# Two transformer layers on one core: the norm roots, the split order and GpSimd's products at three stage beginnings

## What is computed

```python
def rmsnorm(x, g):
    return x * rsqrt(mean(x * x, axis=-1) + EPS) * g

h = h + mix @ w_o                                             # end of the first layer's mixing
n = rmsnorm(h, g_ffn)
h = h + (silu(n @ w_gate) * (n @ w_up)) @ w_down              # feed-forward 1
x = rmsnorm(h, g_final)                                       # between the layers
hn = rms_norm(x, attn_norm_g); proj = hn @ w_in_2             # second layer begins
h = x + mixed @ w_out_2
hn = rms_norm(h, ffn_norm_g)
h = h + (silu(hn @ w_gate_2) * (hn @ w_up_2)) @ w_down_2      # feed-forward 2
```

## Time and profile before

| | |
|---|---|
| median of 3 runs | 797.39 us (796.32 to 799.02) |
| profiled execution | 796.91 us, its span 795.2 us |
| granted TensorE clock, mean | 0.996 |
| busy: PE, PEld | 757.7 us (95%), 680.0 us |
| busy: DVE, ACT, POOL | 530.1, 421.0, 73.9 us |
| DMA read | 129.39 MB, 165 GB/s over the span |
| chain that ended last: PE, DVE, ACT, POOL | 58%, 8%, 2%, 1% of the span |

### The profile page before, as it was taken

How to read it: one execution, slowest core, us unless ns; L and a number is a source line. 1 busy time by engine, 2 the same in 40 slices (tenths; PEclk the granted TensorE clock), 3 DMA queues, 4 the chain that set the end, 5 groups by cost and what they waited for, 6 DMA issues and landing times.

```text
span 795.2 us, 12591 instructions
## 1 busy us (share of the span) xinstructions
PE 757.7 (95%) x4989; PEld 680.0 (86%) x4989; DVE 530.1 (67%) x930; ACT 421.0 (53%) x799; POOL 73.9 (9%) x106
## 2 busy tenths in 40 slices
PE   2999999999999998999999998998989999999998
PEld 2999999989989987888888887997768888888886
DVE  5666465766555768777457757687877877547762
ACT  5356655455554446665345546468455555436551
POOL 8000000013022001000000003301500000000000
PEclk9999999999999999999999999999999999999999
DMA  9887636334433465564656563643234655665521
GB/s 289 237 262 236 164 68 185 107 107 116 150 107 134 159 212 164 181 206 167 211 179 192 187 202 98 214 146 114 102 119 145 212 185 186 212 196 175 168 97 54
DMA packets 108410, 132.04 MB, mean 166 GB/s; under 512 B 4267, under 2 KB 97513, under 8 KB 108352
## 3 DMA queue, kind: packets, MB, share of 16 engines
q1 hardware_dynamic: 106048, 126.56, 49.9%
q0 software_dynamic: 2304, 4.68, 2.6%
HBM read 129.39 MB, written 1.84 MB: 165 GB/s over the span
## 4 chain that ended last, share of the span: by engine, by line
PE 58%; DVE 8%; ACT 2%; issue 2%; POOL 1%; POOLq 0%; DVEq 0%
PE B L1480 23%; PE B L1457 19%; PE B L1462 10%; PE B L1441 5%; DVE LO L902 3%; ACT HI L510 1%; POOL SGC L465 1%; DVE AA L908 0%; PE B L1487 0%; PE B L1616 0%; DVE TMP L1358 0%; ACT SGC L830 0%; DVE NW L918 0%; ACT AA L514 0%; DVE ST L1177 0%
## 5 line engine op out<-in xcount | busy, mean ns | idle before, releaser
L902 DVE TENSOR_TENSOR LO<-RAW,HI 128x1024 fp32r<-128x1024 f32 x240 | 282.5, 1212 | 118.1 <-ACT HI L510 117.6
L510 ACT ACTIVATE HI<-RAW 128x1024 fp32r<-128x1024 f32 x240 | 237.8, 1040 | 60.1 <-PE B L1480 55.3
L1457 PE MATMUL B<-AA,HI 128*128 128x512 f32 x704 | 243.8, 399 | 2.6 <-DVE SGC L1191 2.1
L1480 PE MATMUL B<-HI,AA 128*128 128x512 f32 (+1 forms) x800 | 211.6, 350 | 6.4 <-DVE AA L1374 3.8
L1441 PE MATMUL B<-AA,HI 128*128 128x256 f32 (+1 forms) x992 | 186.0, 289 | 3.5 <-DVE LO L902 1.7
L1462 PE MATMUL B<-AA,LO 128*128 128x256 f32 x704 | 183.2, 281 | 0.0
L1480 PEld LDWEIGHTS B<-HI,AA 128*128 128x128 f32 x800 | 141.5, 190 | 26.3 <-DVE AA L1374 4.2
L1441 PEld LDWEIGHTS B<-AA,HI 128*128 128x128 f32 (+1 forms) x992 | 156.4, 193 | 5.7 <-DVE LO L902 2.1
L1457 PEld LDWEIGHTS B<-AA,HI 128*128 128x128 f32 x704 | 126.8, 188 | 27.9 <-DVE SGC L1191 2.7
L1441 PE MATMUL B<-AA,LO 128*128 128x256 f32 (+1 forms) x496 | 141.4, 285 | 0.0
L1462 PEld LDWEIGHTS B<-AA,LO 128*128 128x128 f32 x704 | 132.9, 189 | 8.1
(11 more groups left out here) (276 smaller groups left out, 639.0 us busy)
## 6 DMA issues: line engine op xcount, KB each, us to landing
RAW<-in_w_in SPq DMA_DIRECT2D x30, 1024.0 KB, 6.2
RAW<-in_w_gate SPq DMA_DIRECT2D x22, 1024.0 KB, 5.3
RAW<-in_w_up SPq DMA_DIRECT2D x22, 1024.0 KB, 5.3
RAW<-in_w_down SPq DMA_DIRECT2D x22, 1024.0 KB, 5.0
RAW<-in_w_in SPq DMA_DIRECT2D x9, 512.0 KB, 6.4
RAW<-in_w_attn_out SPq DMA_DIRECT2D x4, 1024.0 KB, 5.3
RAW<-in_w_o SPq DMA_DIRECT2D x4, 1024.0 KB, 5.0
RAW<-in_w_out SPq DMA_DIRECT2D x4, 1024.0 KB, 5.2
```

What stands on the lines that cost most here:

```text
L510: e.activation(pieces(HI, NSPL, i, k), pieces(RAW, NRAW, i, k), ACT.Copy).then_inc(split_hi, 1)
L902: e.tensor_tensor(pieces(LO, NSPL, i, k), pieces(RAW, NRAW, i, k), pieces(HI, NSPL, i, k), ALU.subtract).then_inc(split_lo, 1)
L1457: return e.matmul(dst[:, :], hi[:, t, c0:c0 + 128], flatten(AA[:, ch + t, :, :]), start=(t == 0), stop=(t == nk - 1))
L1480: x = e.matmul(dst, a, w[:, t, c0:c0 + n], start=(first and t == 0 and k == 0), stop=(last and t == nk - 1 and k == 2))
```

## The change

Five things are edited:
1. Four roots (one at the beginning of each feed-forward part, two at the beginning of the second layer) are no longer computed by DVE's `rsqrt`. DVE counts up `mean_sb`, and GpSimd raises the 128x2 tile to the power -0.5 in one instruction (`root`, a new constant tile ROOT), counts up `root_sb`, and DVE goes on. The two roots at the very start of the kernel stay as they were.
2. GpSimd's G2 product waits for `fg_sb` 6 (the third gate unit of feed-forward 1), its two X products wait for `diag_sb` 4 (the diagonals at the beginning of the second layer).
3. In both feed-forward parts the split of unit g+3 for i = 0 moves behind the two banks' copies, on ACT and on DVE.
4. At the beginning of the second layer the split of unit U_TWO+1 moves behind the last two turned halves, on ACT and on DVE.
5. There DVE's split of unit U_TWO+2, whose halves lay between the parts of the root, moves behind the diagonals.

To have semaphores free, `bias_out` and `bias_in` are made one, and so are the pairs of the two gates' semaphores (`gate_pe`, `gate_tanh`, `gate_sb`), with values that go on counting; nothing waits for another event than before by that. The diff without these renamings:

```diff
+        ROOT = sb("ROOT", [128, 2])
...
             e.memset(ones[:, :], 1.0).then_inc(setup, 1)
+            e.memset(ROOT[:, :], -0.5).then_inc(setup, 1)
...
+            def root(n, dst, src):
+
+                e.wait_ge(mean_sb, n)
+                e.tensor_tensor(dst, src, ROOT[:, :], ALU.pow).then_inc(root_sb, 1)
+
...
             e.wait_ge(scaled_sb, 8)
             gain(1, A["attn_norm_g_2"][0, :])
+            e.wait_ge(setup, HALF)
+            root(1, ST[:, 6:8], ST[:, 4:6])
             e.wait_ge(gain_in[0], 32)
             e.wait_ge(gain_in[1], 32)
             e.wait_ge(mix_lo, 8)
+            e.wait_ge(fg_sb, 6)
             e.tensor_tensor(G2, GB[:, 0, :], GB[:, 1, :], ALU.mult).then_inc(gain2, 1)
...
-            e.wait_ge(factor1, 1)
+            root(2, ST[:, 6:8], ST[:, 4:6])
+            root(3, ST[:, 26:28], ST[:, 24:26])
+            e.wait_ge(root_sb, 2)
             e.wait_ge(squares_sb, 16)
             e.wait_ge(final_x, 4)
+            e.wait_ge(diag_sb, 4)
             for t in range(2):
                 e.tensor_scalar(X[:, t, :], TOK[:, t, :], ST[:, 6 + t:7 + t], None, ALU.mult).then_inc(normal_x, 1)
...
             mean(1, bufs[1][:, 0:256], bufs[2], bufs[0])
+            root(4, ST[:, 6:8], ST[:, 4:6])
...
                     g = ffn_unit(first, "gate", i)
                     hi(g + 2)
-                    if i == 0:
-                        hi(g + 3)
...
-                    if i > 0:
-                        hi(g + 3)
+                    hi(g + 3)
...
+                for t in range(2):
+                    turned(12 + 2 * h + t, B[5 + t], 4 * h, t)
                 if h == 1:
                     hi(U_TWO + 1)
-                for t in range(2):
-                    turned(12 + 2 * h + t, B[5 + t], 4 * h, t)
...
-                    if h == 1 and split is not None:
-                        lo(split)
                     if targets:
                         for t in range(2):
                             turned(n + 2 * h + t, B[5 + t], 4 * h, t)
+                    if h == 1 and split is not None:
+                        lo(split)
...
-            def factor(nsq):
+            def factor(nsq, n):
                 e.wait_ge(squares_sb, nsq)
-                own.step(e.scalar_tensor_tensor(ST[:, 4:6], ST[:, 0:4:2], EPS, ST[:, 1:4:2], ALU.add, ALU.add))
-                own.step(rsqrt(ST[:, 6:8], ST[:, 4:6], 2))
-                own.wait()
+                e.scalar_tensor_tensor(ST[:, 4:6], ST[:, 0:4:2], EPS, ST[:, 1:4:2], ALU.add, ALU.add).then_inc(mean_sb, 1)
+                e.wait_ge(root_sb, n)
                 diagonals(ST[:, 6:8])
...
                     lo(g + 2)
-                    if i == 0:
-                        lo(g + 3)
...
-                    if i > 0:
-                        lo(g + 3)
+                    lo(g + 3)
...
             e.wait_ge(squares_sb, 16)
-            own.step(e.scalar_tensor_tensor(ST[:, 4:6], ST[:, 0:4:2], EPS, ST[:, 1:4:2], ALU.add, ALU.add))
-            rsqrt(ST[:, 6:8], ST[:, 4:6], 2).then_inc(factor1, 1)
-            lo(U_TWO + 2, 0)
+            e.scalar_tensor_tensor(ST[:, 4:6], ST[:, 0:4:2], EPS, ST[:, 1:4:2], ALU.add, ALU.add).then_inc(mean_sb, 1)
             own.step(e.tensor_tensor(ST[:, 24:26], ST[:, 20:24:2], ST[:, 21:24:2], ALU.add))
-            e.wait_ge(factor1, 1)
+            e.wait_ge(root_sb, 2)
             for _ in range(2):
                 own.wait()
                 own.step(e.tensor_tensor(ST[:, 24:26], ST[:, 24:26], ST[:, 6:8], ALU.mult))
             own.wait()
-            own.step(e.tensor_scalar(ST[:, 24:26], ST[:, 24:26], EPS, None, ALU.add))
-            own.step(rsqrt(ST[:, 26:28], ST[:, 24:26], 2))
-            own.wait()
+            e.tensor_scalar(ST[:, 24:26], ST[:, 24:26], EPS, None, ALU.add).then_inc(mean_sb, 1)
+            e.wait_ge(root_sb, 3)
             e.tensor_tensor(ST[:, 28:30], ST[:, 26:28], ST[:, 6:8], ALU.mult).then_inc(factor2, 1)
-            lo(U_TWO + 2, 1)
             e.wait_ge(factor2, 1)
             diagonals(ST[:, 28:30])
+            lo(U_TWO + 2)
```

More of the change, by code:

```diff
@@ L170, in program @@
         conv_hi, conv_lo = sem("conv_hi"), sem("conv_lo")
[L171 removed]
+        gate_pe, gate_tanh = sem("gate_pe"), sem("gate_tanh")
         co_pe, co_sb = sem("co_pe"), sem("co_sb")
@@ L179, in program @@
         fu_pe, fu_low, fu_sb, ff_sb, ff_hi, ff_lo = (sem(n) for n in ("fu_pe", "fu_low", "fu_sb", "ff_sb", "ff_hi", "ff_lo"))
-        factor1, factor2 = sem("factor1"), sem("factor2")
+        mean_sb, root_sb, factor2 = sem("mean_sb"), sem("root_sb"), sem("factor2")
         tm_pe, tm_sb, fm_pe, fm_sb = sem("tm_pe"), sem("tm_sb"), sem("fm_pe"), sem("fm_sb")
@@ L234, in program @@
         for i in range(4):
-            cols(w1, GBO + 48 + 256 * i, 256, gc_pe, 2 * i + 2)
+            cols(w1, GBO + 48 + 256 * i, 256, gate_pe, 2 * i + 2)
         for i in range(2):
@@ L238, in program @@
         for i in range(4):
-            cols(w1, GBO + 48 + 1024 + 256 * i, 256, ga_pe, 2 * i + 2)
+            cols(w1, GBO + 48 + 1024 + 256 * i, 256, gate_pe, 2 * i + 10)
         for i in range(4):
@@ L397, in _, with gates @@
             e.dma_start(bias_rows.rearrange("h r n -> h (r n)").rearrange("h (r n) -> h r n", n=ROW),
-                        OH[0:4, :].unsqueeze(1).to_broadcast([4, 128, ROW])).then_inc(bias_out, 16)
-            def gates(dst, tanh, done):
+                        OH[0:4, :].unsqueeze(1).to_broadcast([4, 128, ROW])).then_inc(bias_moved, 16)
+            def gates(dst, first):
                 for ch in range(8):
-                    e.wait_ge(tanh, ch + 1)
-                    e.tensor_scalar(dst[:, ch, :], dst[:, ch, :], 0.5, 0.5, ALU.mult, ALU.add).then_inc(done, 1)
+                    e.wait_ge(gate_tanh, first + ch + 1)
+                    e.tensor_scalar(dst[:, ch, :], dst[:, ch, :], 0.5, 0.5, ALU.mult, ALU.add).then_inc(gate_sb, 1)
                     yield
@@ L623, in turned_weights, with gates @@
                 e.activation(PT[:, s % 2, :], B[5 + s % 2][:, :], ACT.Copy).then_inc(pturn_sb, 1)
-            def gates(dst, u, pe, done):
+            def gates(dst, u, first):
                 for i in range(4):
@@ L629, in gates @@
                         ch = 2 * i + c
-                        e.wait_ge(pe, ch + 1)
-                        e.activation(dst[:, ch, :], B[c][:, 0:S], ACT.Tanh, scale=0.5).then_inc(done, 1)
+                        e.wait_ge(gate_pe, first + ch + 1)
+                        e.activation(dst[:, ch, :], B[c][:, 0:S], ACT.Tanh, scale=0.5).then_inc(gate_tanh, 1)
                         yield
@@ L662, in fill @@
                 e.wait_ge(block_lo, 1)
-                yield from gates(SGC, u, gc_pe, gc_tanh)
+                yield from gates(SGC, u, 0)
                 u = U_FILL + 12
@@ L671, in fill @@
                 e.wait_ge(o_pe, o_no(13))
-                yield from gates(SGA, u, ga_pe, ga_tanh)
+                yield from gates(SGA, u, 8)
             filler = fill()
@@ L1225, in _ @@
             lo(U_FF1 + 1)
-            factor(8)
+            factor(8, 1)
             ffn(U_FF1, 0, 1)
@@ L1297, in second_most @@
                 if i == 0:
-                    e.wait_ge(bias_in, 16)
+                    e.wait_ge(bias_moved, 32)
                 if i >= 2:
@@ L1410, in _ @@
             lo(U_FF2 + 1)
-            factor(20)
+            factor(20, 4)
             ffn(U_FF2, 22, 3)
@@ L1623, in turn_outputs, with gates @@
                     turn(4 + 2 * h + t, TOK[:, t, halves(h)], 5 + t)
-            def gates(u, pe, tanh):
+            def gates(u, first):
                 for ch in range(8):
-                    take(ch % 2, tanh, ch + 1)
-                    stationary(u + ch // 2, 128 * (ch % 2), B[ch % 2][:, 0:S], 0, ch % 2 == 0).then_inc(pe, 1)
+                    take(ch % 2, gate_tanh, first + ch + 1)
+                    stationary(u + ch // 2, 128 * (ch % 2), B[ch % 2][:, 0:S], 0, ch % 2 == 0).then_inc(gate_pe, 1)
                     yield
@@ L1651, in fill @@
                         yield
-                yield from gates(U_FILL + 8, gc_pe, gc_tanh)
+                yield from gates(U_FILL + 8, 0)
                 e.wait_ge(conv_lo, 4)
@@ L1658, in fill @@
                         yield
-                yield from gates(U_FILL + 14, ga_pe, ga_tanh)
+                yield from gates(U_FILL + 14, 8)
             e.wait_ge(q_sb, 8)
```

17 lines of the change are left out of this document (8 added, 9 removed).

## The result

The changed kernel takes 790.55 us (median of 4 runs, 790.15 to 790.96), the kernel before beside it 796.99 us (4 runs, 796.32 to 799.02): a ratio of 0.9915, 95% interval 0.9896 to 0.9934, so 5.3 to 8.3 us less. The forecast was 791.5 us.

A forecast was written before the change was run, and what follows sets the result against it. PE, busy for 95% of the 795.2 us span, bounds the kernel, so its waits count. Gains of 2.69 + 0.73 + 2.56 - 0.15 = 5.83 us from 796.91, with 0.48 added for the median, give 791.5 us; range 789.8 to 795.3.

The forecast's parts named there:

- Feed-forward 1: At its beginning the diagonals end at 305.42 + p; PE's waits before spread and gate unit 1 go, gain 2.69 us.
- The step on gate unit 1: Feed-forward 1: with only two half splits ahead of the bank B0 sum, the 1.35 us wait goes if p is under 3.4.
- G2's new place: Near 330 us in feed-forward 1, G2 keeps DVE out for up to 2.8 us; never late, costed at nothing.
- Feed-forward 2: At its beginning the bank B0 sum comes earlier and PE's wait before gate unit 1 goes: gain 0.73 us.
- Turned halves: Second layer's beginning: copies go ahead of U_TWO+1's split; PE's wait of 2.56 us goes, but for 0.1 at most.
- The roots of the second layer: Second layer's beginning: U_TWO+2's split ends at 499.2 + 2p + w; 2p + w must stay under 1.7 us.
- p: Time of one power on POOL at each of the four moved roots, taken as 0.5 us.
- w: Second layer's beginning: time the X products keep DVE out of U_TWO+2's split, taken as 0.85 us, bounds 0 and 1.7.
- the term of -0.15 us: A new PE wait of 0.15 us at U_TWO+2 in the second layer, from 2p + w = 1.85, taken off the gain.
- The price formula for a slow power: Rival at all four roots: above 2.7 us waits grow by p - 2.7, 2p - 0.85, p - 2.5; gain 12.0 - 4p; chance 0.08.
- The rivals: X products hold DVE out fully, 0.17; power moderately long, 0.12; time comes back elsewhere, 0.06; slow power routine, 0.08.
- The sum: Whole kernel: the gains at the three stage beginnings, 2.69 + 0.73 + 2.56 - 0.15 = 5.83 us.

The follow-up runs named there:

- the roots alone: The kernel before with only the four roots moved to GpSimd, order of before, neither added wait: 796.6 us, ratio 0.9976 to the kernel before.
- the run with four powers: The changed kernel with each of the four roots computed four times in series on GpSimd: 796.87 us, ratio 0.9986 to the kernel before.
- the second (7.3 to 9.4): The changed kernel, with nothing further changed, measured once more against the kernel before: 790.23 us, ratio 0.9895.

## Why the prediction was right, step by step

- **Feed-forward 1, right.** The mean takes 0.15 us, both waits are gone. The diagonals end at 308.19, 1.54 us after the mean's start at 306.65; the formula gives 0.15 + 0.22 + 0.72 + 0.48 = 1.57 us. The gain was 3.17 and not 2.69 us, since a wait costs more than its bracket here. The step on gate unit 1 gave its wait to edit 3; the runs show that the short root with G2 held back does it alone and that edit 3 does it alone too. The number does not depend on it, since both are in the change.
- **G2's new place, right in effect.** That G2 would keep DVE out near 330 us at no cost is what happened (L1204 takes 2.94 us for two there, and PE does not wait). What the prediction did not say is what G2 would have done in its old place behind the power: the roots alone keep 1.52 us of the two waits for it. The held product is part of the change and not of the prediction's reasons for the gain.
- **Feed-forward 2, right.** 0.96 us instead of 0.73, for the same reason.
- **Turned halves, right.** 2.57 us of 2.56. PE has no gap at all, where up to 0.1 was allowed.
- **The roots of the second layer, right, with two errors that in part cancel.** p is 0.7 and not 0.5 us, and w, the time that the X products take from U_TWO+2's split, is 0 and not 0.85. DVE's part of U_TWO+2 ends at 496.49 + 2.35 = 498.8; the formula with p = 0.7 and w = 0 gives 500.6 in the time of the execution before, 499.5 in this one's, which is 1.1 us ahead there. So 0.7 us more slack than was worked out, and the term of -0.15 us fell away. The size of w was right and its place was wrong. An X product does keep DVE out for some 0.85 us, but here the first half of U_TWO+2's split begins before it and the second follows without a break, both at their usual 1.22 us; the time falls on the first half of U_TWO+3's split (1.53 us instead of 0.68), for which PE does not wait. With the roots alone, where the second half of U_TWO+2's split begins 0.12 us behind the first X product, that half takes 2.07 us instead of 1.22: so w can fall on this split. (In the earlier trace rows the row of 1.01 us is two instructions, of 0.82 and 0.16 us, so the first hold there was 0.66 us.) POOL's two products grew from 6.58 to 9.65 us. The rule of the Trainium skill (SBUF — State Buffer, "Who interferes with whom") that the one that holds the port locks out the other for its whole instruction is borne out for the TENSOR_TENSOR G2; the TENSOR_SCALAR X products, 4.71 and 4.95 us long, did not keep DVE's splits out for their whole length.
- **The price formula for a slow power, right but for that slack.** With p = 3.04 us it gives waits of 0.34, 0.54 and (2p - 1.7, w = 0) 4.4 us, in all 5.3; the trace has 0.35, 0.27 and 3.65, the last one shorter by the same 0.7 us of slack. The formula's break-even is at 3.0 us, and there the run with four powers lies, with a ratio of 0.9986. It loses some clock besides, so part of that agreement is chance.
- **The rivals.** None took place at the power's real length. The Trainium skill (GPSIMD Engine Reference, "Instruction dispatch") has about 6 us for the first call of a freshly loaded routine; the first power here takes 0.72 us, the later ones 0.69 to 0.72.
- **The sum.** 5.83 forecast; by the starts of rows 6.7. The missing part is 0.24 us for each of three waits and the 0.15 that was taken off for nothing. The first comparison (5.3 to 8.3 us) holds 5.83, the second (7.3 to 9.4) does not: the sum has no term for the clock, and the gain was somewhat larger than forecast.

## What to carry to other kernels

A chain of small instructions on a busy engine between a reduction and the engine that waits for it can be cut by one instruction of an idle engine, if the tile is narrow: here 0.7 us and 0.2 us for two hops against 2.0. Look at what then follows on the helping engine: its next large instruction starts at the very moment at which the first engine goes on, and it can take back what was won (here DVE's diagonals took 2.63 us instead of 0.48 behind G2). Two edits that remove the same wait are worth one, and an edit that removes a wait on one engine (the turned halves) may need another (the roots) to keep its gain, so edits are measured alone and left out one at a time.

## What was not expected of the hardware

A power on GpSimd costs 0.4 us and 0.16 us for each column over 128 partitions (0.70, 1.02, 5.46 us for 2, 4, 32 columns). Two GpSimd products of 128x1024 by a column took from 6.2 us (the roots alone) to 9.65 us, and longest where DVE's splits were under way when they began; 16 of 24 such products (two in each of the twelve profiles) held one DVE instruction up, for 0.7 to 0.9 us. A row that merges instructions of two widths hides this: the four half splits under them take 4.40 us together, 1.10 us on average, which looks like no hold at all beside 1.22 us for one of 128x1024. TensorE's granted clock falls to 0.50 for some 3.4 us or twice that at a time, one to four times in a profiled execution. Each of the 21 such dips in the twelve profiles (without the fall at the very end of an execution) begins inside a wait of PE of 0.9 us or more or at most 1.3 us behind its end, though these stretches make only about 20 us of each span; most such waits (88 in all) have no dip. The sums that this costs (1.7 to 6.8 us of full clock) are of the size of the scatter between executions of one kernel (1 to 5 us).
